# A decoder step on one core: first stage in another order, with the norm's gain row spread by TensorE

## What is computed

```python
xn = rmsnorm(x, norm1_g)                  # x * rsqrt(mean(x*x) + EPS) * norm1_g, 1024 channels
proj = xn @ w_in
q, k, v, glu, gates = split(proj)
u = glu_a * sigmoid(glu_b)                # the GLU, 1024 channels
# later: three groups of dilated window attention on q, k, v;
c = causal_dwconv(u_ext, conv_w, conv_b)  # 31 taps for each channel; u_ext = 30 rows of history, then u
# layernorm, swish, projections, gates, w_o, and a squared-ReLU MLP of width 4096
```

## Time and profile before

| | |
|---|---|
| time of three runs | 1098.77, 1109.07, 1109.81 us; median 1109.07 us |
| profiled execution | 1107.68 us; span in the trace 1105.8 us |
| TensorE busy, share of the span | 1022.5 us, 92% |
| VectorE, ScalarE, GpSimd busy | 636.0, 507.1, 161.0 us |
| chain that ended last | PE 77%, ACT 7%, DVE 5% |

### The profile page before, as it was taken

One profiled execution on the slowest core, in us unless ns is written; L12 is line 12 of the kernel. 1 busy time (PEld: TensorE's weight loads), 2 busy tenths in 40 slices (PEclk: granted clock), 3 DMA queues, 4 the chain that ended last, 5 costly groups with the idle time before them and its releaser, 6 DMA issues.

```text
span 1105.8 us, 22024 instructions
## 1 busy us (share of the span) xinstructions
PE 1022.5 (92%) x8334; PEld 991.9 (90%) x8334; DVE 636.0 (58%) x896; ACT 507.1 (46%) x762; POOL 161.0 (15%) x178
## 2 busy tenths in 40 slices
PE   2999999999999999985875999999999999999998
PEld 2899999899899899875874898999999999999998
DVE  3577779568658768758967925554442224443221
ACT  4333367667668558643640234444541114453221
POOL 4000000220220220238255013110000000000000
PEclk8899999999999999998886989999999999999999
DMA  6233585484575556336673432344444444444442
GB/s 175 77 95 91 195 324 164 138 292 147 179 239 193 188 193 218 109 107 234 137 228 99 160 114 72 93 131 140 130 140 143 142 129 131 140 142 143 137 158 67
DMA packets 173010, 169.57 MB, mean 153 GB/s; under 512 B 7850, under 2 KB 162762, under 8 KB 170231
## 3 DMA queue, kind: packets, MB, share of 16 engines
q1 hardware_dynamic: 163271, 138.49, 39.2%
q0 software_dynamic: 9664, 30.08, 8.6%
HBM read 159.19 MB, written 64.86 MB: 203 GB/s over the span
## 4 chain that ended last, share of the span: by engine, by line
PE 77%; ACT 7%; DVE 5%; issue 5%; DMA 3%; SPq 1%; POOL 1%; DVEq 0%; ACTq 0%; POOLq 0%
PE ps L673 68%; DMA w_raw<-in_w_conv_out_dram 2%; PE ps L613 1%; ACT w_high L984 1%; PE ps L600 1%; PE ps L785 1%; DMA chan_rows<-in_norm_g_dram 1%; ACT L907 1%; DVE ln_sum L1377 1%; DVE w_low L1256 1%; PE ps L569 1%; POOL gate_a L1699 1%; PE ps L777 1%; PE ps L587 1%; PE ps L562 1%
## 5 line engine op out<-in xcount | busy, mean ns | idle before, releaser
L1256 DVE TENSOR_TENSOR w_low<-w_raw,w_high 128x1024 fp32r<-128x1024 f32 x152 | 208.0, 1368 | 308.0 <-ACT w_high L984 308.0
L984 ACT ACTIVATE w_high<-w_raw 128x1024 fp32r<-128x1024 f32 x152 | 161.1, 1060 | 424.8 <-PE ps L673 407.9
L673 PE MATMUL ps<-x_high,w_high 128*128 128x260 f32 x1600 | 330.8, 288 | 7.9 <-ACT far_b L972 2.6
L673 PE MATMUL ps<-x_high,w_low 128*128 128x260 f32 x1600 | 323.6, 284 | 0.0
L673 PE MATMUL ps<-x_low,w_high 128*128 128x260 f32 x1600 | 323.4, 284 | 0.0
L673 PEld LDWEIGHTS ps<-x_high,w_high 128*128 128x128 f32 x1600 | 248.3, 190 | 15.6 <-issue 9.8
L673 PEld LDWEIGHTS ps<-x_high,w_low 128*128 128x128 f32 x1600 | 248.2, 190 | 0.0
L673 PEld LDWEIGHTS ps<-x_low,w_high 128*128 128x128 f32 x1600 | 248.0, 190 | 0.0
L1161 DVE SCALAR_TENSOR_TENSOR conv<-u_in,chan,conv x240 | 168.1, 749 | 10.2 <-DVE conv L1161 7.9
L673 PE MATMUL ps<-hid_high,w_high 128*128 128x260 f32 x512 | 103.6, 284 | 0.0
L673 PE MATMUL ps<-hid_high,w_low 128*128 128x260 f32 x512 | 103.1, 283 | 0.0
(11 more groups left out here) (247 smaller groups left out, 1167.6 us busy)
## 6 DMA issues: line engine op xcount, KB each, us to landing
w_raw<-in_w_in_dram SPq DMA_DIRECT2D x68, 512.0 KB, 4.2
w_raw<-in_w_ff_dram SPq DMA_DIRECT2D x64, 512.0 KB, 4.1
out_dram<-in_cache_v_dram SPq DMA_DIRECT2D x64, 256.0 KB, 5.8
out_dram<-in_cache_k_dram SPq DMA_DIRECT2D x64, 256.0 KB, 4.1
out_dram<-in_cache_k_dram SPq DMA_DIRECT2D x8, 1022.0 KB, 7.2
out_dram<-in_cache_v_dram SPq DMA_DIRECT2D x8, 1022.0 KB, 7.0
kbuf<-in_cache_k_dram POOLq DMA_DIRECT2D x2, 2048.0 KB, 14.7
qbuf<-new_qkv POOLq DMA_DIRECT2D x4, 1024.0 KB, 7.1
```

The lines of the kernel that those rows point to most:

```text
L673: mm = pe.matmul(out[:, h, :], w[:, k, n0:n0 + P], x[:, k0 + k, h * HT:(h + 1) * HT], start=(first and k == 0 and n == 0), stop=(last and ...
L984: act.activation(w_high[a % 2][:, :, :], w_raw[a % 2][:, :, :], ACT.Copy).then_inc(cast_done, 1)
L1256: dve.tensor_tensor(w_low[a % 2][:, :, :], w_raw[a % 2][:, :, :], w_high[a % 2][:, :, :].bitcast(F32), ALU.subtract).then_inc(split_done, 1)
```

## The change

The first stage is written again, in the code of all five engines.

- SP loads the 8 sample tokens first, then the four blocks. The broadcast of `norm1_g` is gone from its queue, and so are the loads of `chan_rows` and `state_rows`.
- GpSimd loads `norm1_g` as one row of one partition (`gain_row`) with its first instruction. TensorE spreads it to 128 partitions by two matmuls with a row of ones, into PSUM banks 6 and 7, and `x_scale` reads it there. `x_scale` writes in place; `xn_tok` is gone.
- GpSimd also loads `chan_rows` (five DMAs) and `state_rows`, behind the first constants and ahead of its other constants and the 12 loads of `qk_gain`.
- Mean and EPS go into the Sqrt activation as scale and bias; VectorE's `x_variance` is gone. The table with Sqrt is loaded ahead of the first wait.
- Each block goes through square, scale, transpose, round and subtract in turn, samples first. Unit 0 is computed one half of the columns at a time; the first half waits for blocks 0 to 2 and the samples, the second for block 3.
- The first pass of the GLU loop is written out. TensorE transposes `chan_rows` and the first half of `state_rows` behind unit 0 and the second half behind unit 1. VectorE makes the tables ahead of the `split` for `j` = 1, multiplies the history ahead of that of `j` = 2, and sums it ahead of that of `j` = 3.

Cut to its core:

```diff
         @block.sync
+            sp.dma_start(x_tok[0:TS, NB, :], x_sample.rearrange("b s d -> (b s) d")).then_inc(x_in[NB], 16)
             for b in range(NB):
                 sp.dma_start(x_tok[:, b, :], x_prompt[0, b * P:(b + 1) * P, :]).then_inc(x_in[b], 16)
-                if b == 0:
-                    sp.dma_start(gain1[:, :], norm1_g.to_broadcast([P, D])).then_inc(gain_in, 16)
...
-            sp.dma_start(chan_rows[0:CW, :], conv_w[0]).then_inc(chan_in, 16)
-            for r, vec in ((C_BIAS, conv_b), (C_LNG, conv_ln_g), (C_LNB, conv_ln_b), (C_N2, norm2_g)):
-                sp.dma_start(chan_rows[r:r + 1, :], vec).then_inc(chan_in, 16)
-            sp.dma_start(state_rows[:, :, :], ...).then_inc(state_in, 16)
         @block.tensor
+                if half_ready is not None:
+                    for h in range(2):
+                        half_ready(h)
+                        for k in range(nk):
+                            for n, (w, x) in enumerate(((wh, high), (wh, low), (wl, high))):
+                                mm = pe.matmul(out[:, h, :], w[:, k, 0:P], x[:, k, h * HT:(h + 1) * HT], ...)
...
+            pe.wait_ge(gain_in, 16)
+            for h in range(2):
+                mm = pe.matmul(ps[:, 6 + h, :], one_row[:, :], gain_row[:, h * 512:(h + 1) * 512], start=True, stop=True)
+            mm.then_inc(gain_full, 1)
...
+            for j in range(4):
+                if j >= 2:
+                    pe.wait_ge(state_done, j - 1)
+                pe.wait_ge(u_done, j // 2 + 1)
+                unit(U_GLU + j, 0, 0, pair(j), x_high, x_low,
+                     half_ready=(lambda h: pe.wait_ge(x_low_done, 4 + h)) if j == 0 else None).then_inc(unit_done, 1)
+                if j == 0:
                     pe.wait_ge(chan_in, 16 * 5)
...
+                    pe.wait_ge(state_in, 16)
+                    state_part(0)
+                if j == 1:
+                    pe.wait_ge(chan_done, 1)
+                    state_part(1)
         @block.scalar
+            act.preload_act_table_set("sqrt_and_others")
+                act.activation(x_rstd[:, i:i + 1], x_ss[:, i:i + 1], ACT.Sqrt, scale=1.0 / D, bias=eps_col[:, :])
...
+            for j in range(4):
+                cast(U_GLU + j + 2, 0, 0)
+                if j == 0:
                     act.wait_ge(chan_tr, 1)
+                    act.activation(chan[:, :, :], ps[:, 6, 0:KT * NCV], ACT.Copy).then_inc(chan_done, 1)
+                if j < 2:
+                    act.wait_ge(state_tr, j + 1)
+                    act.activation(state[:, 4 * j:4 * j + 4, :, :]..., ps[:, 4 + 2 * j:6 + 2 * j, 0:480], ACT.Copy)
+                if j % 2:
+                    glu_gate(j, 0, 0)
         @block.vector
+            dve.wait_ge(gain_full, 1)
+            x_scale(4)
+            x_scale(0)
+            x_scale(1)
...
+            for j in range(4):
+                if j == 1:
+                    tables()
+                    dve.wait_ge(chan_done, 1)
+                if j == 2:
+                    dve.wait_ge(state_done, 2)
+                    dve.tensor_tensor(state[:, :, :, :], state[:, :, :, :], taps_b, ALU.mult).then_inc(sconv, 1)
+                if j == 3:
+                    dve.wait_ge(sconv, 1)
+                    dve.tensor_reduce(sc, state[:, :, :, :], AX.X, ALU.add).then_inc(sconv, 1)
+                glu_unit(j, 0, 0)
         GpSimd's block
+            pool.dma_start(gain_row[:, :], norm1_g).then_inc(gain_in, 16)
             link(pool.memset(ident[:, :], 0.0))
...
+            pool.dma_start(chan_rows[0:CW, :], conv_w[0]).then_inc(chan_in, 16)
...
+            pool.dma_start(state_rows[:, :, :], ...).then_inc(state_in, 16)
```

More of the change, by code:

```diff
@@ L655, in _, with unit @@
         def _(pe):
-            def unit(a, b, it, out, high, low, ready=None, k0=0, first=True, last=True, cols=None, part=None):
+            def unit(a, b, it, out, high, low, ready=None, k0=0, first=True, last=True, cols=None, part=None, half_ready=None):
                 if not part:
@@ L666, in unit @@
                     wl = wl[:, :, :].rearrange("p k n -> p (k n)").rearrange("p (k n) -> p k n", k=4)
+                if half_ready is not None:
[3 more added lines that the diff above has]
+                            for n, (w, x) in enumerate(((wh, high), (wh, low), (wl, high))):
+                                mm = pe.matmul(out[:, h, :], w[:, k, 0:P], x[:, k, h * HT:(h + 1) * HT],
+                                               start=(k == 0 and n == 0), stop=(k == nk - 1 and n == 2))
+                    return mm
                 for k in (range(nk) if part is None else (part,)):
@@ new lines, in _, with glu_gate @@
+            x_square(4)
+            x_square(0)
+            x_square(1)
+            act.wait_ge(x_tr, 1)
+            act.activation(x_high[:, :, TP:T], ps[:, 0, 0:KT * TS].rearrange("p (k c) -> p k c", k=KT), ACT.Copy).then_inc(x_high_done, 1)
+            x_square(2)
+            x_round(0)
+            x_square(3)
+            x_round(1)
+            cast(0, 0, 0)
+            x_round(2)
+            x_round(3)
+            cast(1, 0, 0)
+            def glu_gate(j, b, it):
+                done(U_GLU + j, b, it)
+                act.wait_ge(u_done, at_(j // 2 + 1, b // 2, it))
+                act.activation(halves(glu_sig[:, j // 2, :]), pair(j), ACT.Sigmoid).then_inc(glu_sig_done, 1)
@@ L1020, in _ @@
+            with act.Fori(1, 4) as it:
                 for j in range(4):
@@ L1022, in _ @@
                     if j % 2:
[L1023 to L1025 removed]
+                        glu_gate(j, 4, it)
             with act.Fori(0, 2) as tt:
@@ L1284, in _ @@
[L1284 to L1288, removed]
-                dve.reciprocal(x_rinv[:, i:i + 1], x_rstd[:, i:i + 1]).then_inc(x_rs, 1)
[L1290 to L1298, removed]
+                dve.wait_ge(x_sd, (i + 1) % 5 + 1)
@@ L1299, in _ @@
+            dve.tensor_tensor(x_low[:, :, TP:T], ps[:, 0, 0:KT * TS].rearrange("p (k c) -> p k c", k=KT),
+                              x_high[:, :, TP:T].bitcast(F32), ALU.subtract).then_inc(x_low_done, 1)
+            x_scale(2)
+            x_part(dve, 0)
+            x_scale(3)
+            x_part(dve, 1)
             split(0, 0, 0)
+            x_part(dve, 2)
             x_part(dve, 3)
-            x_part(dve, 4)
             split(1, 0, 0)
-            dve.wait_ge(qkg_in, 16 * 12)
-            dve.tensor_scalar(qk_gain[:, 0:G], qk_gain[:, 0:G], -E ** -0.5, None, ALU.mult).then_inc(mask_done, 1)
```

161 lines of the change are left out of this document (75 added, 86 removed).

## The result

Over 20 runs each, the changed kernel took 1102.97 us (median; 1093.58 to 1107.74) and the kernel before 1108.8 us (1098.77 to 1111.97). The ratio is 0.9949, with a 95% interval of 0.9928 to 0.9969: 5.6 us faster, within 3.4 and 8.0. Forecast were 8.4 us. The profiled execution took 1105.45 us.

The account below looks back on a forecast made before the run. TensorE was taken to bound the kernel (92% of the span), so its start of units and waits count. Gain 15.0 - 6.6 = 8.4 us took the profiled 1107.68 to 1099.3; from the median, 1100.7 us, range 1094.5 to 1107.

Parts of the forecast that it names:

- first term: First stage: unit 0 ends at 26.4 us instead of 41.39, 15.0 us earlier (18.0 to 10.2).
- Gain row: Start of first stage: load lands at 3.9 us, two spreading matmuls take 2.1, row in PSUM at 6.0 (5.35 to 8.4).
- a gain row after 8 us: Stated sign, in the first stage, that the prediction would be wrong: the gain row lands after 8 us.
- VectorE's chain: First stage: VectorE's scales, x_part, x_low and split from the gain row to unit 0's possible start, 12.3 us.
- TensorE's wait behind `chan_rows`: Before unit 0 in the old kernel: TensorE stands from 12.72 to 23.06 us behind the last chan_rows load.
- Sharing of the queues: First stage, block 3: the history's 960 KB on the other queue compete with its load, 1.0 us (0 to 1.8).
- second rival: First stage: two queues alternate, holding up block 3 and first weights 3.2 us; gain 6.2 us, 1102.9; chance 0.15.
- Unit 0's clock: Unit 0: takes 7.1 us as before; 5.77 at the higher clock throughout, 8.7 with the lower for 5.75 us.
- What the first pass gives back: First GLU pass: moved transposes, ScalarE's copy and VectorE's history work start unit 6 6.6 us later, or 7.5, counted from unit 0's end.
- slack of 0.04 us: GLU before unit 6: VectorE's split ends at 70.15 us, TensorE's units 0 to 5 at 70.19, so added VectorE work delays unit 6.
- rival in which VectorE catches up: Rival listed first, GLU: only 2.3 us of transposes come back; gain 12.7 us, 1096.4; chance 0.16.
- The rows come late: Rival, end of unit 0: TensorE waits for late history; gain gone at 35 us, 1120 at 46; chance 0.07.

Follow-up runs that it names:

- rows later: Changed kernel, but GpSimd issues the chan_rows and state_rows loads only once the first weights have landed; unit 0 started at 21.87 us, unit 15 ended at 120.10.
- gain broadcast: Changed kernel with the gain again broadcast by a 512 KB DMA on SP's queue behind block 0, no TensorE spreading; unit 0 started at 24.46 us.
- gain row alone: Changed kernel with the gain row loaded on SP's queue ahead of the samples instead of on GpSimd's; unit 0 started at 20.89 us, unit 15 ended at 119.32.

## Why the prediction was right, and where its terms were not

The direction, the size (a difference within 1%) and the time (1102.97 in 1094.5 to 1107) were as forecast, and so was the mechanism in outline: unit 0 starts earlier, and the first GLU pass gives part of it back. That the time came so near is in part luck. Both terms were too large, and since one is taken from the other, their errors took each other's place: 15.0 - 6.6 = 8.4 forecast, 10.1 - 3.4 = 6.7 measured at the end of the GLU. The 10.1 lies at the late end of the first term (18.0 to 10.2), the 3.4 far below both values of the second (6.6 and 7.5).

- *Gain row*, forecast in PSUM at 6.0 us with a late end of 8.4; it was 9.36, outside that bound. Issue was 0.5 us later than I took it, the landing 1.6 us later in all, and the spread 3.75 us where I had 2.1 from the earlier trace rows: each matmul of 512 columns shows as two. This is the step that failed outright, and by the prediction's own sign, a gain row after 8 us: the load had landed by 5.5, but VectorE had the row at 9.36.
- *VectorE's chain* of 12.3 us: 12.4 where nothing else interfered (rows later), so right.
- *TensorE's wait behind `chan_rows`* was read as 12.72 to 23.06 us. That is the transfer on the chain; TensorE stood 7.05 us of it.
- *Sharing of the queues*, 1.0 us on block 3: the block did land later with the rows issued early, 8.8 us after its issue against 7.3 in *rows later*, but VectorE came to it so late that it did not wait. Loads on one queue did hold up those on the other, as in the second rival, and it was the first weights that they struck: these landed at 19.4 us, against 12.3 with the rows issued later. That the queues take every second turn was my assumption, and no run shows how they share. In the changed kernel's trace unit 0 waited for the weights (1.2 us on VectorE), in two other executions with the same loads it did not. That the rival's 1102.9 is almost the measured time is chance: it counts 3.2 us for what cost at most 1.2. The trace before has a stretch with both queues at work too: 512 KB of weights that SP issued at 141.01 us, 0.4 us after 2 MB on GpSimd's queue, took 6.5 us to land, and those issued between 45 and 130 us took 3.7 to 5.5.
- *Unit 0's clock*: 7.1 us forecast, 8.3 measured (7.6 in two other executions), inside the ends of 5.8 and 8.7. The granted clock was 0.50 from 22 to 27 us and 1.00 from 28 us on.
- *What the first pass gives back*: `u_in` came 42.53 - 31.31 = 11.2 us after unit 0's end, exactly as worked out, and the product and sum took 4.1 us of the chain. But the `split` of unit 6 ended at 32.1, not 35.4: I had carried the old loop's 0.93 us for a tap over into code that is no longer a loop. Sixteen taps at 0.78 us are 2.4 us less, and the steps around `u_in` gained some too. The "slack of 0.04 us" was read with the 0.18 us between taps as work. What was given back is 2.3 us of transposes behind units 0 and 1 and 1.1 us of waiting ahead of unit 6, where the forecast had 2.3 (a part of it ScalarE's copy) and 4.3. So the rival in which VectorE catches up and only the 2.3 us come back was nearer than the forecast here, for a reason that it did not name. The expected wait at unit 5 did not occur.
- *The rows come late* did not occur: the history landed 12.8 us after its issue, by 19 us, and was needed at 31.
- *The range*: with its own first stage early, the first rival gives 18.0 - 2.3 = 15.7 us, or 1093.4, which lies below the 1094.5 that is said to take it in.
- *All later stages move forward as they are*: by the runs they nearly do (5.6 of 6.7 us, within the interval). In the two profiled executions only 2.0 us are left at 732 us, but executions of one code differ there by 14 us. Nor do two differences of this pair of traces say more. TensorE's granted clock from 660 to 680 us was 1.00 before and 0.91 after, but 1.00 in *gain broadcast*. A wait for weights behind 138 us is new in the chain after, but the chains of the other nine traces have it too, that of the old code with the rows on GpSimd among them. What makes the later stages scatter stays open.

## What to carry to other kernels

When a wait is taken away, look for what is next in line: here the first weights stood up to 2 us behind VectorE's chain from the gain row. Rows later alone left unit 0 at 21.87 us, which other executions reach without it, the gain row alone at 20.89, and both at 18.85. Loads moved to a second queue still delayed those on the first here (the first weights landed 13.7 to 16.1 us after issue with the rows issued early, 8.7 to 9.1 with them late); bulk that is needed late should be issued after what is needed first. And a cost per instruction that was read inside the hardware loop (0.93 us for a tap) did not hold for the same instructions written out (0.78 us): read what stands between them.

## What was not expected of the hardware

- A dependent VectorE tap, which takes 0.75 us, came every 0.93 us inside the hardware loop (changed kernel, second pass) and every 0.78 us written out.
- A load of one 4 KB row as GpSimd's first transfer took 3.9 us to land, where I had 2.3 us from a later and larger one; on SP's queue it had landed by 2.64 us.
- 24 transposes ahead of unit 0, which compute nothing, saved 1.5 to 2.2 us of it (6.1 us instead of 7.6 to 8.3).
